# Down projection: the loads of the token tiles move from SP's queue to ScalarE's

## The chip, the cores and the metric

One Trainium2 chip; the kernel runs on 1 of its cores, and what counts is the device time of one launch in microseconds. TensorE multiplies, VectorE, ScalarE and GpSimd compute beside it, and SP (SyncE) issues DMAs. Each engine runs its own instruction list; semaphores order them. The time before is 1884.01 us, the median of 3 runs from 1882.34 to 1884.18.

## The reference, cut to what matters

The whole is one layer of a decoder for 1024 new tokens and 8 sampled ones, 1032 in all, in float32: a feed-forward half-step, a mixer (sliding-window attention beside HGRN2), and a second feed-forward half-step. The change touches the second product of both half-steps:

```
D_MODEL, D_FF = 1024, 2816

def half_step_ffn(x, g_pre, g_post, w_gu, w_down):
    h = rms_norm(x, g_pre)
    gate, up = jnp.split(h @ w_gu, 2, axis=-1)
    y = (jax.nn.silu(gate) * up) @ w_down
    return x + 0.5 * rms_norm(y, g_post)
```

`h @ w_down` is (1032 x 2816) times (2816 x 1024).

## The kernel before, in words

**Precision.** Every float32 factor is split in two parts of a shorter type: ScalarE copies the high part (`w_hi`, `x_hi`, also called `t_hi`), VectorE subtracts it from the original to get the low part (`w_lo`, `x_lo`). A product is three matmuls: high x high, high x low, low x high (L778 to L780).

**The down projection.** Tokens stand in three groups of 344. The product is computed with fewer multiplications in Strassen's manner: eleven streams, each a product of some combination of weight quarters with some combination of token quarters. Both kinds of combinations were formed in the gate and up stage and written to DRAM: token tiles to `spill_h`, weight sums to `spill_s`; some weights come directly from `w_down`. A stream has 11 blocks, so there are 121 blocks per half-step; a block is a weight tile of 128 x 512 (256 KB), a token tile of 128 x 344 (172 KB) and 12 matmuls. Two blocks make a pair: 61 pairs, numbered 0 to 60, the last with one block. There are two half-steps (`f` is 0 or 1), and so two such stages, from about 477 to 710 us and from about 1638 to 1870 us of the profiled execution.

**Buffers.** Raw weights of a pair go to `raw[p % 3]`, three slots; raw tokens to `t_raw`, eight tiles or four pairs deep. Their parts have as many slots. A pair's four transfers, two of weights and two of tokens, all count on one semaphore, `blocks_in[p % 4]`.

**The order of the work, written out by hand.** TensorE runs the blocks in order. In front of a pair it waits for `ab_low`, VectorE's count of finished pairs of low parts, and after each block it counts up `d_step`. ScalarE's loop (L1477) calls `high_parts(p)`: first the split of the tokens (L1417), then the split of the weights (L1406). Both wait in `landed(p)` until all four transfers of the pair are there; the weight split also waits on `d_step` until TensorE has finished pair p-3, whose slot it takes. Work of other kinds stands behind some pairs (`behind`, L1468 to L1476): copies of finished sums out of PSUM, squares and inverse roots for the norms, the input parts of the stage that follows. VectorE's loop does the low parts in the same manner (L2148, L2141).

**The loads.** All DMAs of this stage are issued by SP (L485 to L510). For each pair from 3 on, SP waits until the low parts of pair p-3 are done, so that the weight slot is free, issues the two weight loads (L461), waits until TensorE has finished pair p-4, whose token slot is taken, and issues the two token loads (L467). At a few pairs it also issues the last spills of the stage before (`last_out`), and from pair 12 to pair 27 six loads of the residual stream (L508); before pairs 4, 10, 11 and 20 it waits until those spills have been written that the coming tiles read (`t_out`, `odd_out`, `sums_out`). The tokens of pairs 1 to 3 are issued ahead of this loop (L484).

Of the kernel before, what the change touches and what calls it, by code (L numbers as in the profile page):

```python
# [21 lines left out]
KT = D_MODEL // P  # L22
# [13 lines left out]
FFN_STEPS = HT // 2  # L36
# [9 lines left out]
PAIR_STEPS = FFN_STEPS - 1  # L46
# [13 lines left out]
BLOCK_PAIRS = (BLOCKS + 1) // 2  # L60
LAST_PAIR = BLOCK_PAIRS - 1
COUNTED = BLOCKS - 1 + len((2, 3, 4, 5))
# [84 lines left out]
def tokens_of(k):  # L147

    s, i = divmod(k, FFN_STEPS)
    return (B11, T2, B21, T1, T3, B22, T4, E0, O0, E0, O0)[s], i  # L150


def slot_user(p):

    return p - 3


def pair_blocks(p):

    return range(2 * p, min(2 * p + 2, BLOCKS))  # L160
# [20 lines left out]
def build(nc, ins, outs):  # L181
    ctx = ExitStack()
    with ctx:
        sems = {}

        def sem(name):
            sems[name] = ctx.enter_context(nc.semaphore(name))
            return sems[name]
# [5 lines left out]
        def put(name, shape, dt, offset=None):  # L194
            size = (2 if dt == BF16 else 4) * int(np.prod(shape[1:]))
            if offset is None:
                offset = at[0]
                at[0] += (size + 31) // 32 * 32
            assert offset + size <= end, (name, offset + size - end)
            return nc.alloc_sbuf_tensor_at(name, shape, dt, offset=offset)  # L200
# [45 lines left out]
        t_raw = put("t_raw", [P, KT, GW], F32, x_at + 4 * NG * KT * GW)  # L246
# [86 lines left out]
        blocks_in = [sem(f"blocks_in{s}") for s in range(4)]  # L333
# [16 lines left out]
        S = sems  # L350
# [28 lines left out]
        def _(sp):  # L379
# [9 lines left out]
            def steps(n0, f, w_gu, w_down, x, first_load, late):  # L389

                done, hd, sums = FFN_STEPS * f, ins[f"spill_h{f}"], ins[f"spill_s{f}"]
# [62 lines left out]
                def weights_in(p):  # L454
                    for k in pair_blocks(p):
                        direct, summed_, i = weights_of(k)
                        src = w_down[direct[0]][:, direct[1]] if direct else sums[i][:, summed_]
                        if p == LAST_PAIR:
                            sp.dma_start(e_raw[:], src).then_inc(blocks_in[p % 4], 16)
                        else:  # L460
                            sp.dma_start(raw[p % 3][:, HALF * (k % 2):HALF * (k % 2 + 1)], src).then_inc(blocks_in[p % 4], 16)  # L461

                def tokens_in(p):
                    for k in pair_blocks(p):
                        op, i = tokens_of(k)
                        to, landed = (t_raw[:, k % KT], blocks_in[p % 4]) if p else (first_raw[:, k], S["first_in"])
                        sp.dma_start(to, hd[i][:, op]).then_inc(landed, 16)  # L467
# [17 lines left out]
                for p in range(3, BLOCK_PAIRS):  # L485
                    sp.wait_ge(S["ab_low"], BLOCK_PAIRS * f + slot_user(p) + 1)
                    if p == 4:
                        sp.wait_ge(S["t_out"], 16 * (done + PAIR_STEPS + f))
                        sp.wait_ge(S["sums_out"], 16 * (done + PAIR_STEPS + f) + 16)
                    if p == 10:  # L490
                        sp.wait_ge(S["t_out"], 16 * (done + FFN_STEPS + f))
                        sp.wait_ge(S["sums_out"], 16 * (done + FFN_STEPS + f) + 16)
                    if p == 11:
                        sp.wait_ge(S["odd_out"], 16 * (done + FFN_STEPS))
                    if p == 20:
                        sp.wait_ge(S["t_out"], 16 * (done + FFN_STEPS + f + 1))
                        sp.wait_ge(S["sums_out"], 16 * (done + FFN_STEPS + f + 1) + 16)
                    weights_in(p)
                    if p > 3:
                        sp.wait_ge(S["d_step"], COUNTED * f + 2 * (p - 4) + 2)  # L500
                        tokens_in(p)
                    if p in last_out:
                        last_out[p]()
                    for g, at_ in ((2, 12), (1, 18), (0, 24)):
                        for a in range(2):
                            if p == at_ + 3 * a:
                                t = slice(KT // 2 * a, KT // 2 * (a + 1))
                                sp.dma_start(resid[:, g, t], x[g][:, t]).then_inc(resid_full[g], 16)  # L508
                    if p in late:
                        late[p]()  # L510
# [7 lines left out]
            sp.dma_start(ident[:], ins["ident"]).then_inc(S["consts_in"], 16)  # L518
            sp.dma_start(head_ones[:], ins["head_ones"]).then_inc(S["consts_in"], 16)
            steps(0, 0, ins["w_gu1"], ins["w_down1"], ins["x"], 2, {53: lambda: store(0, outs["x1"], 0, 2)})  # L520
            sp.wait_ge(S["ab_low"], 58)
            sp.dma_start(raw[0][:], ins["w_in"][0]).then_inc(raw_full[0], 16)
# [742 lines left out]
        def _(act):  # L1265
# [8 lines left out]
            def square(n, src):  # L1274
                prior = [m for m in norms[:norm_no[n]] if sq_no[m] == sq_no[n]]
                if prior:
                    act.wait_ge(S["ss_done"], norm_no[prior[-1]] + 1)
                nc.scalar.activation(sq_bufs[sq_no[n]][:], src, ACT.Square, scale=D_MODEL ** -0.5).then_inc(S["sq_done"], 1)
# [27 lines left out]
            def ffn(u0, f, slot_uses, b):  # L1306
# [89 lines left out]
                def weights_high(p):  # L1396

                    landed(p)
                    if p == LAST_PAIR:
                        nc.scalar.activation(e_hi[:], e_raw[:], ACT.Copy).then_inc(S["ab_high"], 1)  # L1400
                        return
                    if p < 3:
                        act.wait_ge(S["p_done"], PRODUCTS * (last_pair + p // 2) + P4)
                    else:
                        act.wait_ge(S["d_step"], COUNTED * f + 2 * slot_user(p) + 2)
                    nc.scalar.activation(w_hi[p % 3][:], raw[p % 3][:], ACT.Copy).then_inc(S["ab_high"], 1)  # L1406

                def tokens_high(p):

                    if p:  # L1410
                        landed(p)
                        src = t_raw[:, 2 * p % KT:2 * p % KT + len(pair_blocks(p))]
                    else:
                        act.wait_ge(S["first_in"], 32 * (f + 1))
                        act.wait_ge(S["p_done"], PRODUCTS * (last_pair + 1) + UP)
                        src = first_raw[:]
                    nc.scalar.activation(t_hi[:, 2 * p % KT:2 * p % KT + len(pair_blocks(p))], src, ACT.Copy).then_inc(S["ab_high"], 1)  # L1417

                def high_parts(p):

                    tokens_high(p)
                    weights_high(p)
# [19 lines left out]
                def x_hi_half(g, a):  # L1442
                    r = rank_of(g)
                    if a:
                        act.wait_ge(S["x_new"], NG * b + r + 1)
                    else:
                        act.wait_ge(S["x_half_new"], NG * f + r + 1)
                    if g == 0:
                        act.wait_ge(S["d_step"], COUNTED * (f + 1))
                    high(b, g, a)  # L1450
# [10 lines left out]
                def gained(a):  # L1461
                    if a == 0:
                        act.wait_ge(S["y2_sq"], SQUARED + 1)
                    for m in range(KT // 2 * a, KT // 2 * (a + 1)):
                        st = nc.scalar.activation(y[:, 0, m], y[:, 0, m], ACT.Copy, scale=GAIN_F[b][:, m:m + 1])
                    st.then_inc(S["y_gained"], 1)
# [4 lines left out]
                if b == 0:  # L1471
                    behind.update({46: lambda: x_hi_half(2, 0), 47: lambda: x_hi_half(2, 1), 50: lambda: square(("S", 1, 2), resid[:, 2]),
                                   53: lambda: x_hi_half(1, 0), 54: lambda: x_hi_half(1, 1), 58: lambda: inverse(("S", 1, 2)),
                                   56: lambda: square(("S", 1, 1), resid[:, 1]), 59: square_lead})
                else:
                    behind.update({55: square_lead, 57: lambda: gained(0)})  # L1476
                for p in range(1, BLOCK_PAIRS):  # L1477
                    high_parts(p)
                    if p == 4:
                        act.preload_act_table_set("natural_log_exp_and_others")  # L1480
                    if p in behind:
                        behind[p]()
# [339 lines left out]
            square_x(2)  # L1822
            inverse(("S", 2, 2))
            ffn(U_FFN2, 1, [30, 30, 19, 11], 2)


# [1012 lines left out]
```

## Time and profile before

| what | before |
|---|---|
| median of 3 runs | 1884.01 us |
| profiled execution, own time | 1883.94 us |
| its span in the trace | 1882.1 us |
| TensorE busy | 1865.9 us (99%) |
| VectorE busy | 1371.2 us (73%) |
| ScalarE busy | 802.3 us (43%) |
| GpSimd busy | 35.1 us (2%) |
| mean DMA rate over the span | 158 GB/s |

The times of the table are of one execution, taken by the hardware profiler. Busy time is the union of an engine's instructions; issuing a DMA and waiting on a semaphore do not count as busy. Matmuls are pipelined: each is shown with some 320 ns, while the next one starts some 157 ns after it. "Idle before" is the time for which an engine stood still just before an instruction, and the releaser is what ended it. The share of the DMA engines is a mean over 16 of them.

### The profile page before, as it was taken

What the parts mean: (1) busy time and instruction counts of PE and PEld (TensorE: products, weight loads), DVE (VectorE), ACT (ScalarE), POOL (GpSimd) and SP (SyncE); (2) the same over time, 40 slices, a digit from 0 to 9 for tenths busy, and PEclk for the clock granted to TensorE, in tenths of its full rate; (3) what the DMA queues carried; (4) which work ended last, traced back from release to release, by engine and by line L of the source; (5) the groups of instructions that cost most, each with busy time, mean ns of one, the idle gap of its engine ahead of it and who ended that gap; (6) DMA issues with size and microseconds to landing.
All of it is one profiled execution on the core that took longest, in us unless ns stands there. A gap on an engine that the chain in (4) does not pass through costs nothing.

```text
span 1882.1 us, 36299 instructions
## 1 busy us (share of the span) xinstructions
PE 1865.9 (99%) x14325; PEld 1825.5 (97%) x14325; DVE 1371.2 (73%) x2132; ACT 802.3 (43%) x1278; POOL 35.1 (2%) x27
## 2 busy tenths in 40 slices
PE   9999999999999999999999999999999999999997
PEld 8999999999999999999898899999999999999997
DVE  7876767766756885578888678986776667766784
ACT  6423232323545673146565646522232223354553
POOL 0000000000000000000101100000000000000000
PEclk9999999999999999999999999999999999999999
DMA  5253433344798783210110465243434433598775
GB/s 191 79 191 123 149 127 141 123 162 155 260 313 254 224 270 106 64 40 25 36 30 31 143 242 171 85 171 126 145 123 154 149 140 126 178 315 294 227 242 181
DMA packets 115883, 296.60 MB, mean 158 GB/s; under 512 B 13200, under 2 KB 44824, under 8 KB 111160
## 3 DMA queue, kind: packets, MB, share of 16 engines
q1 hardware_dynamic: 115624, 294.93, 46.1%
q8 instruction: 84, 1.38, 0.3%
q14 instruction: 31, 0.25, 0.0%
q10 hardware_dynamic: 144, 0.03, 0.0%
HBM read 221.25 MB, written 73.00 MB: 156 GB/s over the span
## 4 chain that ended last, share of the span: by engine, by line
PE 94%; DVE 3%; ACT 1%; issue 1%; DMA 0%; DVEq 0%; SPq 0%; ACTq 0%
PE PS L669 9%; PE PS L671 9%; PE PS L670 9%; PE PS L778 8%; PE PS L780 8%; PE PS L779 8%; PE PS L678 5%; PE PS L679 5%; PE PS L680 5%; PE PS L901 2%; PE PS L902 2%; PE PS L903 2%; PE PS L642 2%; PE PS L644 2%; PE PS L643 2%; PE PS L1092 2%
## 5 line engine op out<-in xcount | busy, mean ns | idle before, releaser
L778 PE MATMUL PS<-x_hi,w_hi 128*128 128x344 f32 x960 | 309.2, 322 | 0.0
L780 PE MATMUL PS<-x_hi,w_lo 128*128 128x344 f32 x960 | 306.9, 320 | 0.0
L779 PE MATMUL PS<-x_lo,w_hi 128*128 128x344 f32 x960 | 306.6, 319 | 0.0
L1309 ACT ACTIVATE silu_g<-silu_g 128x344 f32<-128x344 f32 x92 | 45.0, 491 | 443.8 <-DVE silu_g L2121 258.9
L678 PE MATMUL PS<-x_hi,w_hi 128*128 128x344 f32 x640 | 204.7, 320 | 0.0
L679 PE MATMUL PS<-x_lo,w_hi 128*128 128x344 f32 x640 | 204.3, 319 | 0.0
L680 PE MATMUL PS<-x_hi,w_lo 128*128 128x344 f32 x640 | 203.8, 318 | 0.0
L778 PEld LDWEIGHTS PS<-x_hi,w_hi 128*128 128x128 f32 x960 | 180.4, 188 | 0.9
L2148 DVE TENSOR_TENSOR x_lo<-t_raw,x_hi 128x688 fp32r<-128x688 f32 x120 | 104.1, 867 | 105.9 <-ACT x_hi L1417 105.3
L779 PEld LDWEIGHTS PS<-x_lo,w_hi 128*128 128x128 f32 x960 | 180.3, 188 | 0.8
L780 PEld LDWEIGHTS PS<-x_hi,w_lo 128*128 128x128 f32 x960 | 180.3, 188 | 0.0
L1417 ACT ACTIVATE x_hi<-t_raw 128x688 fp32r<-128x688 f32 x120 | 92.7, 773 | 185.9 <-DMA t_raw<-spill_h 185.0
L1991 DVE TENSOR_TENSOR s_lo<-s_raw,s_hi 128x512 fp32r<-128x512 f32 x160 | 106.8, 688 | 82.2 <-ACT s_hi L1335 82.2
L1335 ACT ACTIVATE s_hi<-s_raw 128x512 fp32r<-128x512 f32 x160 | 100.8, 630 | 152.9 <-DVE s_raw L2098 138.9
L2141 DVE TENSOR_TENSOR w_lo<-raw,w_hi 128x1024 fp32r<-128x1024 f32 x120 | 146.8, 1224 | 13.0 <-ACT w_hi L1406 8.0
L669 PE MATMUL PS<-x_hi,w_hi 128*128 128x344 f32 x480 | 153.6, 320 | 0.9 <-DVE h_even L2118 0.7
L670 PE MATMUL PS<-x_sum,s_hi 128*128 128x344 f32 x480 | 153.9, 321 | 0.0
L671 PE MATMUL PS<-x_sum,s_lo 128*128 128x344 f32 x480 | 153.8, 320 | 0.0
L669 PE MATMUL PS<-x_sum,s_hi 128*128 128x344 f32 x480 | 153.7, 320 | 0.0
L671 PE MATMUL PS<-x_hi,w_lo 128*128 128x344 f32 x480 | 153.2, 319 | 0.0
L670 PE MATMUL PS<-x_lo,w_hi 128*128 128x344 f32 x480 | 152.8, 318 | 0.0
L1842 DVE TENSOR_TENSOR w_lo<-raw,w_hi 128x1024 fp32r<-128x1024 f32 x111 | 135.3, 1219 | 11.3 <-ACT w_hi L1272 7.0
(309 smaller groups left out, 4439.4 us busy)
## 6 DMA issues: line engine op xcount, KB each, us to landing
raw<-in_w_gu SPq DMA_DIRECT2D x88, 512.0 KB, 4.3
t_raw<-spill_h SPq DMA_DIRECT2D x238, 172.0 KB, 2.9
raw<-in_w_down SPq DMA_DIRECT2D x152, 256.0 KB, 3.6
d_raw<-in_w_down SPq DMA_DIRECT2D x44, 512.0 KB, 6.1
raw<-spill_s SPq DMA_DIRECT2D x88, 256.0 KB, 4.4
spill_s<-d_sum SPq DMA_DIRECT2D x20, 1024.0 KB, 5.1
spill_h<-T SPq DMA_DIRECT2D x20, 688.0 KB, 3.1
spill_h<-h_odd SPq DMA_DIRECT2D x22, 516.0 KB, 2.7
```

Of the source, the lines that this page charges most:

```text
L669: nc.tensor.matmul(PS[:, bank, :GW], wh[:, c], vh[:, k], start=(start and k == 0), stop=False, skip_group_check=not start)
L670: nc.tensor.matmul(PS[:, bank, :GW], wh[:, c], vl[:, k], start=False, stop=False, skip_group_check=not start)
L671: mm = nc.tensor.matmul(PS[:, bank, :GW], wl[:, c], vh[:, k], start=False, stop=(k == KT // 2 - 1), skip_group_check=not start)
L678: nc.tensor.matmul(PS[:, 7, :GW], wh, vh, start=(k == 0), stop=False)
L679: nc.tensor.matmul(PS[:, 7, :GW], wh, vl, start=False, stop=False)
L680: mm = nc.tensor.matmul(PS[:, 7, :GW], wl, vh, start=False, stop=(k == KT - 1))
L778: nc.tensor.matmul(PS[:, bank, :GW], hi[:, c], vh, start=opens, stop=False, skip_group_check=again)
L779: nc.tensor.matmul(PS[:, bank, :GW], hi[:, c], vl, start=False, stop=False, skip_group_check=again)
L780: mm = nc.tensor.matmul(PS[:, bank, :GW], lo[:, c], vh, start=False, stop=closes, skip_group_check=again)
L1842: nc.vector.tensor_tensor(w_lo[s][:], raw[s][:], w_hi[s][:].bitcast(F32), ALU.subtract)\
L1991: nc.vector.tensor_tensor(s_lo[k][:], s_raw[k][:], s_hi[k][:].bitcast(F32), ALU.subtract).then_inc(S["s_low"], 1)
L2141: return nc.vector.tensor_tensor(to[:], src[:], hi[:].bitcast(F32), ALU.subtract)
```

## The change

SP no longer issues the token loads of pairs 4 to 60, and no longer waits for `t_out`, `odd_out` and `d_step` there. ScalarE issues them: in the loop of pair p, after `high_parts(p)` and ahead of what stands behind the pair, it waits on `d_step` until TensorE has finished pair p-3 (that is (p+1)-4) and issues the two token loads of pair p+1 in its own queue. The waits for the spills move with them; that for the first `t_out` stands at pair 5, the first that reads such a tile. The token loads of pairs 1 to 3, the weight loads and all other transfers stay with SP. The four transfers of a pair still count on the same semaphore, and no size of a transfer or a buffer is changed.

```
                 for p in range(3, BLOCK_PAIRS):
                     sp.wait_ge(S["ab_low"], BLOCK_PAIRS * f + slot_user(p) + 1)
                     if p == 4:
-                        sp.wait_ge(S["t_out"], 16 * (done + PAIR_STEPS + f))
                         sp.wait_ge(S["sums_out"], 16 * (done + PAIR_STEPS + f) + 16)
                     if p == 10:
-                        sp.wait_ge(S["t_out"], 16 * (done + FFN_STEPS + f))
                         sp.wait_ge(S["sums_out"], 16 * (done + FFN_STEPS + f) + 16)
-                    if p == 11:
-                        sp.wait_ge(S["odd_out"], 16 * (done + FFN_STEPS))
                     if p == 20:
-                        sp.wait_ge(S["t_out"], 16 * (done + FFN_STEPS + f + 1))
                         sp.wait_ge(S["sums_out"], 16 * (done + FFN_STEPS + f + 1) + 16)
                     weights_in(p)
-                    if p > 3:
-                        sp.wait_ge(S["d_step"], COUNTED * f + 2 * (p - 4) + 2)
-                        tokens_in(p)
...
+                hd = ins[f"spill_h{f}"]
+
+                def tokens_in(p):
+
+                    done = FFN_STEPS * f
+                    if p == 5:
+                        act.wait_ge(S["t_out"], 16 * (done + PAIR_STEPS + f))
+                    if p == 10:
+                        act.wait_ge(S["t_out"], 16 * (done + FFN_STEPS + f))
+                    if p == 11:
+                        act.wait_ge(S["odd_out"], 16 * (done + FFN_STEPS))
+                    if p == 20:
+                        act.wait_ge(S["t_out"], 16 * (done + FFN_STEPS + f + 1))
+                    act.wait_ge(S["d_step"], COUNTED * f + 2 * (p - 4) + 2)
+                    for k in pair_blocks(p):
+                        op, i = tokens_of(k)
+                        act.dma_start(t_raw[:, k % KT], hd[i][:, op]).then_inc(blocks_in[p % 4], 16)
+
                 for p in range(1, BLOCK_PAIRS):
                     high_parts(p)
+                    if 3 < p + 1 < BLOCK_PAIRS:
+                        tokens_in(p + 1)
                     if p == 4:
                         act.preload_act_table_set("natural_log_exp_and_others")
                     if p in behind:
```

## Rows read from the trace of the kernel before

**Rows 1.** Page, part 1: busy us (share of the span) and instructions.
```profile
PE 1865.9 (99%) x14325; PEld 1825.5 (97%) x14325; DVE 1371.2 (73%) x2132; ACT 802.3 (43%) x1278; POOL 35.1 (2%) x27
```

**Rows 2.** Windows: busy time of each engine, PEclk, DMA share, GB/s.
```profile
480.00:590.00 110.00, 110.00 (x700) 109.95 (x699) 71.24 (x74) 54.20 (x65) 0.00 (x0) 1.00 0.89 293
590.00:700.00 110.00, 110.00 (x694) 109.21 (x693) 94.25 (x111) 73.20 (x88) 0.00 (x0) 1.00 0.76 238
1640.00:1750.00 110.00, 110.00 (x700) 109.95 (x699) 71.62 (x75) 55.21 (x64) 0.00 (x0) 1.00 0.89 291
...
1750.00:1858.00 108.00, 108.00 (x683) 107.40 (x682) 80.41 (x87) 61.02 (x71) 0.00 (x0) 1.00 0.77 242
```

**Rows 3.** Page, part 5: ScalarE's split of tokens, busy and idle time before.
```profile
L1417 ACT ACTIVATE x_hi<-t_raw 128x688 fp32r<-128x688 f32 x120 | 92.7, 773 | 185.9 <-DMA t_raw<-spill_h 185.0
```

**Rows 4.** Timeline of SP, 564 to 580 us: start, us, issues.
```profile
564.10 0.81 SPq L467 DMA_DIRECT2D t_raw<-spill_h  x2
...
567.89 2.21 SPq L467 DMA_DIRECT2D t_raw<-spill_h  x2
570.14 0.43 SPq L508 DMA_DIRECT2D resid<-in_x  x1
...
571.67 0.82 SPq L467 DMA_DIRECT2D t_raw<-spill_h  x2
...
575.46 0.81 SPq L467 DMA_DIRECT2D t_raw<-spill_h  x2
...
579.27 1.01 SPq L467 DMA_DIRECT2D t_raw<-spill_h  x2
```

**Rows 5.** Timelines of ScalarE and (last row) VectorE, 567 to 583 us.
```profile
567.55 0.78 ACT L1417 ACTIVATE x_hi<-t_raw 128x688 fp32r<-128x688 f32 x1 [0.52 <-DMA t_raw<-spill_h]
...
572.06 0.78 ACT L1417 ACTIVATE x_hi<-t_raw 128x688 fp32r<-128x688 f32 x1 [2.79 <-DMA t_raw<-spill_h]
...
578.30 0.78 ACT L1417 ACTIVATE x_hi<-t_raw 128x688 fp32r<-128x688 f32 x1 [4.51 <-DMA t_raw<-spill_h]
578.98 1.04 ACT L1406 ACTIVATE w_hi<-raw 128x1024 fp32r<-128x1024 f32 x1
580.53 0.78 ACT L1417 ACTIVATE x_hi<-t_raw 128x688 fp32r<-128x688 f32 x1 [0.51 <-DMA t_raw<-spill_h]
...
582.85 0.78 ACT L1417 ACTIVATE x_hi<-t_raw 128x688 fp32r<-128x688 f32 x1 [0.59 <-DMA t_raw<-spill_h]
...
580.06 1.22 DVE L2141 TENSOR_TENSOR w_lo<-raw,w_hi 128x1024 fp32r<-128x1024 f32 x1
```

**Rows 6.** DMA issues, 480 to 590 us: count, KB each, us to landing.
```profile
raw<-spill_s SPq DMA_DIRECT2D x44, 256.0 KB, 4.4
t_raw<-spill_h SPq DMA_DIRECT2D x58, 172.0 KB, 3.7
resid<-in_x SPq DMA_DIRECT2D x6, 688.0 KB, 5.8
```

**Rows 7.** Timelines of SP and VectorE at the start of the stage.
```profile
484.73 0.80 SPq L467 DMA_DIRECT2D t_raw<-spill_h  x2
...
496.10 0.80 SPq L467 DMA_DIRECT2D t_raw<-spill_h  x2
...
491.88 1.23 DVE L2141 TENSOR_TENSOR w_lo<-raw,w_hi 128x1024 fp32r<-128x1024 f32 x1
```

**Rows 8.** The DMA issue of ScalarE: ns min/median/max, first and last start.
```profile
L1507 ACTq DMA_DIRECT2D vecs<-in_vecs x1: 387/387/387, 0.9 to 0.9; - x1
```

**Rows 9.** Timeline of ScalarE, 680 to 683 us; no idle time in brackets.
```profile
680.21 1.99 ACT L1303 ACTIVATE x_hi<-resid,vecs 128x344 fp32r<-128x344 f32 x4
682.10 0.76 ACT L1417 ACTIVATE x_hi<-t_raw 128x688 fp32r<-128x688 f32 x1
```

**Rows 10.** Landing of t_raw in 480:590, then 590:700, then 1640:1750.
```profile
DMA to landing us min/median/max: 2.4/3.7/6.2
...
DMA to landing us min/median/max: 2.2/2.5/6.4
...
DMA to landing us min/median/max: 2.3/3.4/6.4
```

## The prediction

> **What bounds the kernel now.** I read the page's busy table first: TensorE is busy for 99% of the span and ScalarE for 43% [rows 1]. Then I cut both down projections into a first and a second stretch: in each TensorE is busy for all of its 110 us at a granted clock of 1.00, which is the 2.4 GHz level, and the waits of TensorE list nothing there [rows 2]. So inside the stage that the change touches there is no microsecond to win; whatever the edit does can only be hidden or cost time. The same rows show where the next limit stands: the DMA engines are at 0.89 in the first stretch (293 GB/s) and at 0.76 in the second. The grouped list then shows that ScalarE's split of token tiles has 185.9 us of idle time ahead of it, 185.0 of them until tokens land [rows 3]. This is the load that moves.
>
> How tight it is, from the timelines. SP issues the tokens of one pair at 564.10, 567.89, 571.67, 575.46 and 579.27 us, every 3.79 us, which is TensorE's time for a pair, since that wait counts its steps [rows 4]. ScalarE splits those pairs at 567.55, 572.06, 578.30, 580.53 and 582.85 [rows 5], so from the first issue of a pair to its split took 3.45, 4.17, 6.63, 5.07 and 3.58 us, mean 4.58. The 6.63 lies behind a resid load of 688 KB [rows 4, 6]. Tokens are issued when TensorE starts on the pair three before, that is 3 x 3.79 = 11.37 us ahead of use. The pair split at 578.30 has its low part done at 580.06 + 1.22 = 581.28 [rows 5], and TensorE starts on it at 571.67 + 11.37 = 583.04: 1.8 us of room in the worst of these. From split to low part done is 2.98 us. At the start of the stage (issue 484.73, low part done 493.11, needed at 496.10) the room is 3.0 us [rows 7].
>
> **The change, part by part.**
>
> Removed from SP: two token issues and three kinds of waits per pair. SP is nobody's limit, and its loads of weights now go out when the low part of pair p-3 is done, without standing behind the wait for a TensorE step. They come earlier. Cost and gain nothing: the tokens, not the weights, are what ScalarE waits for [rows 3].
>
> Added to ScalarE: 2 issues for each of 57 pairs in each of 2 projections. The one issue that ScalarE makes before took 0.387 us [rows 8]; 2 x 0.39 = 0.78 us a pair, on an engine that splits for 0.78 + 1.04 us of every 3.79 and idles for most of the rest [rows 5]. Hidden by that idle time; without cover it would be 0.78 x 114 = 89 us of ScalarE, not of TensorE. The spill waits (t_out, odd_out) count transfers issued many pairs before: nothing. The wait for TensorE's step in front of tokens p+1 has the same threshold as that of the weight split of p, which has just passed: nothing. Queued behind the added waits are the copies, squares and inverses of the stage, and they come after the issue.
>
> Moved, and this decides: before, SP issues tokens p+1 when TensorE has finished a pair, whether or not tokens p have landed, so two or three loads are in flight. After, the issue of p+1 stands behind both splits of p, and both of these wait for the landing of p. So only one token load is ever in flight, and the stage gets a loop of its own: issue, land, hand over both splits, issue again. If the loop L is under 3.79 us TensorE still sets the pace; above it every pair takes L - 3.79 out of the room, and then out of TensorE.
>
> L is D, from the first issue to the split, plus the step from split to the next issue. Bounds of that step: near zero if ScalarE's queue runs on while its splits compute, and 0.68 + 1.04 = 1.72 us if the issue waits for the end of the weight split [rows 5]. Rows speak for the first: a split starts at 682.10 without any gap behind activations that began at 680.21, although its wait for landing and others stand between them, and in rows 5 the weight split starts 0.68 us after a token split that lasts 0.78; ScalarE's waits are passed ahead of the work [rows 9]. I take 0.2 us: 0.1 for the hand-over and the rest for issues of 0.39 in place of 0.33.
>
> The Trainium skill (Perfetto Trace Analysis, section "Per-engine timelines") says that an ACT instruction is pushed into a wait queue and that the sequencer is then free, while a hardware DMA is worked off on the sequencer itself. Nothing in the trace of before shows a DMA behind a running activation, so no run here shows it yet; by this rule the step is the small one, by its opposite the third rival holds.
>
> D has bounds too. Below: in the second stretch the median landing is 2.5 us; with 0.37 between the two issues D = 2.87, L = 3.07, and nothing is lost there: under 3.79 it even gives room back. Above: D = 4.58 as in the sample of the first stretch, whose median landing is 3.7 (3.4 in the second projection) [rows 10]. Between them it hangs on the queues. The excess of 4.58 - 2.87 = 1.71 us came in one queue, where tokens wait for all that was issued before them. In a queue of their own they share the engines instead. At 293 GB/s for a share of 0.89 the engines move 329 GB/s when full [rows 2]; the 344 KB of a pair take 1.07 us alone and up to twice that beside a busy SP queue. In the first stretch SP's queue has 512 KB of weights a pair and 6.4 MB of resid loads and spills [rows 6]. With the full overlap of 1.07 I take D = 2.87 + 1.1 = 3.97 and L = 4.17 for the first projection: 0.38 us a pair over the 27 pairs (4 to 30) of the first stretch is 10.3, less the 3.0 of room: 7.3 us of TensorE. For the second projection, with landings shorter by 0.3, L = 3.87 and 0.08 x 27 = 2.2 stays within the room. Sum: +7.3 us.
>
> The Trainium skill (DMA: Bandwidth & Descriptors, "Issuing engines are not separate DMA queues") speaks against the change: loads issued from several engines interleave on the same 16 engines, and a second issuer saves only issue time. By it there is no bandwidth to win; no row of before shows two busy queues at once.
>
> The profiled execution took 1883.94 us for a span of 1882.1, and the median of the runs is 1884.01, so a term of the trace goes onto the median as it is: 1884.0 + 7.3 = 1891.3, say 1891.5.
>
> **The rivals.**
>
> Hidden altogether, the not-slower side. It decides at L = 3.79 in the first stretch, with 3.0 us of room for the sum. If sharing costs the tokens 0.7 us, not 1.1, L = 3.77. A bulk transfer delayed two or three overlapping token loads before and delays only one after. For: the minima of landing are 2.2 to 2.4 us even there [rows 10]. Against: the share of 0.89. Time: 1884, within 2.
>
> Landings stay as they were. If a second queue does not shorten the tokens' wait at all, L = 4.58 + 0.2 = 4.78 in the first projection: 0.99 x 27 - 3.0 = 23.7 us; in the second 0.69 x 27 - 3.0 = 15.6. Together +39: 1923. For: the engines are nearly full whoever issues. Against: the slower loop itself would relieve them.
>
> The issue waits for the computing splits. Then L = D + 1.72: 5.69 in the first stretch and 4.59 in the second: 1.9 x 27 + 0.8 x 29 - 3.0 = 71.5 us per projection, 143 in both: 2027. For: the program order. Against: rows 5 and 9.
>
> Faster: only by a tail or a seam that shifts by chance, as TensorE has no idle time here. 1880 at best.
>
> **How the numbers follow.** A difference of 0.2%, 3.8 us, is about the least that can be told from no change. Chances: forecast (some microseconds of stall, in the first stretches alone) 0.45, its own range 1888 to 1906; hidden 0.33; landings as before 0.12; serial issue 0.07; faster 0.03. So faster 0.03, same 0.33, slower 0.64. The range reaches from the hidden case, 1882, to the case of long landings, 1926; the serial case and some of the rest stay outside.
>
> **What would show it.** Right: the tokens' issues on ScalarE's queue start 0.1 to 0.2 us after a token split starts, not 3.79 us apart by TensorE's steps; their pitch in the first stretch is around 4.1 us until TensorE waits for w_lo in single gaps of some tenths, all before the 31st pair; and in the second stretch the pitch falls back to 3.79 with no gap. D there is under 3.6. Wrong: an issue that starts only 1.7 us after the split (then the stall runs through the stage), a D in the first stretch under 3.6 (then nothing is lost), or waits of TensorE anywhere outside the two projections.

## The result, and the profile after

| | before | changed |
|---|---|---|
| median | 1884.08 us | 1956.09 us |
| runs | 4, 1882.34 to 1884.18 | 4, 1955.02 to 1957.65 |
| span of the profiled execution | 1882.1 us | 1955.9 us |

The ratio is 1.0387, 95% interval 1.0374 to 1.0399: slower by 72 us, where 7 were forecast and the range ended at 1926. The direction was right, the size was not.

The page of the changed kernel, busy line (part 1), the two queues that carry the loads (part 3: packets, MB, share of the engines) and two groups of part 5:

```profile
PE 1890.5 (97%) x14325; PEld 1836.2 (94%) x14325; DVE 1372.5 (70%) x2132; ACT 799.2 (41%) x1278; POOL 35.1 (2%) x27
...
q1 hardware_dynamic: 83080, 255.11, 38.1%
q10 hardware_dynamic: 32688, 39.85, 6.6%
...
L770 PE MATMUL PS<-x_hi,w_hi 128*128 128x344 f32 x960 | 319.3, 333 | 49.1 <-DVE w_lo L2153 39.4
...
L1409 ACT ACTIVATE x_hi<-t_raw 128x688 fp32r<-128x688 f32 x120 | 92.8, 773 | 275.6 <-DMA t_raw<-spill_h 274.4
```

The number of instructions is that of before [rows 1]. TensorE has 49.1 us of idle time in front of the first matmul of a pair, where it had none, and its busy time is 24.6 us longer; the sum is the 73.8 us of span. ScalarE's idle time in front of the token split grew from 185.9 [rows 3] to 275.6 us. VectorE and ScalarE do the same work as before.

The windows that answer to [rows 2] (columns: PE, PEld, DVE, ACT, POOL busy, PEclk, DMA share, GB/s), and the waits of TensorE (total, times, longest):

```profile
480.00:590.00 110.00, 98.26 (x588) 94.92 (x588) 57.43 (x60) 43.75 (x52) 0.00 (x0) 0.97 0.76 245
590.00:720.00 130.00, 120.15 (x726) 116.22 (x725) 94.89 (x108) 69.58 (x85) 0.00 (x0) 0.97 0.68 216
1640.00:1750.00 110.00, 102.20 (x630) 100.17 (x629) 64.06 (x82) 43.37 (x55) 0.00 (x0) 0.98 0.69 222
...
PE PS L770 <- DVE w_lo L2153: 39.4, 32, 3.0
PE PS L770 <- ACT root L1279: 9.0, 2, 4.9
```

In the first 110 us of the stage 588 matmuls start, not 700. The DMA engines are less busy than before, 0.76 for 0.89, so they are not at a limit over the stretch as a whole. Besides the waits for low parts there are two of 4 to 5 us for a root that ScalarE computes, of which the prediction said nothing.

The loop itself, on the timeline of ScalarE in the changed kernel (start, us, engine; ACTq is its queue):

```profile
567.49 0.78 ACT L1409 ACTIVATE x_hi<-t_raw 128x688 fp32r<-128x688 f32 x1 [1.30 <-DMA t_raw<-spill_h]
567.58 0.82 ACTq L1485 DMA_DIRECT2D t_raw<-spill_h  x2
568.17 1.04 ACT L1398 ACTIVATE w_hi<-raw 128x1024 fp32r<-128x1024 f32 x1
572.80 0.78 ACT L1409 ACTIVATE x_hi<-t_raw 128x688 fp32r<-128x688 f32 x1 [3.59 <-DMA t_raw<-spill_h]
572.89 0.82 ACTq L1485 DMA_DIRECT2D t_raw<-spill_h  x2
573.48 1.05 ACT L1398 ACTIVATE w_hi<-raw 128x1024 fp32r<-128x1024 f32 x1
577.90 0.78 ACT L1409 ACTIVATE x_hi<-t_raw 128x688 fp32r<-128x688 f32 x1 [3.38 <-DMA t_raw<-spill_h]
...
616.79 0.78 ACT L1409 ACTIVATE x_hi<-t_raw 128x688 fp32r<-128x688 f32 x1 [2.06 <-DMA t_raw<-spill_h]
...
620.88 0.78 ACT L1409 ACTIVATE x_hi<-t_raw 128x688 fp32r<-128x688 f32 x1 [2.35 <-DMA t_raw<-spill_h]
620.97 0.82 ACTq L1485 DMA_DIRECT2D t_raw<-spill_h  x2
...
624.62 0.78 ACT L1409 ACTIVATE x_hi<-t_raw 128x688 fp32r<-128x688 f32 x1 [2.01 <-DMA t_raw<-spill_h]
```

The issue starts 0.09 us after the token split starts (567.58 after 567.49), while that split still runs for 0.7 us and before the weight split starts. The next split follows when the load has landed: 5.31 and 5.10 us later in the first stretch, 4.09 and 3.74 in the second. The pitch is the mean distance of these starts from pair to pair. In the first projection it is 4.76 us for pairs 4 to 30 (480.07 to 608.66, 27 pairs), 4.03 for 31 to 37, 4.19 for 38 to 51 and 5.00 for 52 to 60; in the second it is 4.79, 3.94, 4.24 and 4.56. TensorE needs 3.79.

Where the time went, from the starts of TensorE's first matmul of a pair, against before, each counted from pair 0 (us, first / second projection): by pair 31 +21.9 / +23.4; by pair 38 +23.1 / +24.5; by pair 40 +29.6 / +32.1; by pair 51 +29.6 / +32.1, nothing more; by pair 60 +34.4 / +39.3. The two sum to 73.7, the whole difference of the spans.

### The profile page after: what moved, and what is told of

Its sections match the earlier page's. It is cut to its first block, busy times and chain, and to the rows that moved or that the text cites. A ratio compares the mean times of both kernels' runs of the same rounds, so it can differ in the third digit from the quotient of the medians.

```text
span 1955.9 us, 36305 instructions
## 1 busy us (share of the span) xinstructions
PE 1890.5 (97%) x14325; PEld 1836.2 (94%) x14325; DVE 1372.5 (70%) x2132; ACT 799.2 (41%) x1278; POOL 35.1 (2%) x27
## 4 chain that ended last, share of the span: by engine, by line
PE 74%; DMA 16%; DVE 4%; ACT 2%; ACTq 2%; issue 2%; DVEq 0%; SPq 0%
DMA t_raw<-spill_h 16%; PE PS L661 9%; PE PS L663 9%; PE PS L662 9%; PE PS L670 5%; PE PS L671 5%; PE PS L672 5%; PE PS L770 3%; PE PS L772 2%; PE PS L893 2%; PE PS L771 2%; PE PS L894 2%; PE PS L895 2%; ACTq L1485 2%; PE PS L636 2%; PE PS L634 2%
## 5 line engine op out<-in xcount | busy, mean ns | idle before, releaser
L770 PE MATMUL PS<-x_hi,w_hi 128*128 128x344 f32 x960 | 319.3, 333 | 49.1 <-DVE w_lo L2153 39.4
L770 PEld LDWEIGHTS PS<-x_hi,w_hi 128*128 128x128 f32 x960 | 184.4, 192 | 63.2 <-DVE w_lo L2153 52.1
L1409 ACT ACTIVATE x_hi<-t_raw 128x688 fp32r<-128x688 f32 x120 | 92.8, 773 | 275.6 <-DMA t_raw<-spill_h 274.4
L670 PE MATMUL PS<-x_hi,w_hi 128*128 128x344 f32 x640 | 204.5, 320 | 0.0
L771 PEld LDWEIGHTS PS<-x_lo,w_hi 128*128 128x128 f32 x960 | 184.5, 192 | 0.9 <-issue 0.2
L661 PE MATMUL PS<-x_hi,w_hi 128*128 128x344 f32 x480 | 153.4, 320 | 0.8 <-DVE h_even L2130 0.7
```

Source lines behind the costliest of these rows:

```text
L661: nc.tensor.matmul(PS[:, bank, :GW], wh[:, c], vh[:, k], start=(start and k == 0), stop=False, skip_group_check=not start)
L670: nc.tensor.matmul(PS[:, 7, :GW], wh, vh, start=(k == 0), stop=False)
L770: nc.tensor.matmul(PS[:, bank, :GW], hi[:, c], vh, start=opens, stop=False, skip_group_check=again)
L771: nc.tensor.matmul(PS[:, bank, :GW], hi[:, c], vl, start=False, stop=False, skip_group_check=again)
```

## The experiments

Three theories stood at the start. One-in-flight: the loads of a pair are tied to the landing of the pair before. Shared-engines: two busy queues slow every load. Issue-time: issuing on ScalarE costs ScalarE's time. The count "in flight" needs a word of care. In the kernel before, the tokens of pair p+1 went out before those of pair p had landed for 17 of the 19 pairs 12 to 30 of the first projection, but for only 3 of the 21 pairs 31 to 51 (13 and 1 in the second projection). What the change adds everywhere is the tie: the next issue can't come before this landing.

**The issue ahead of the splits** (`ahead_of_split`). Only the order in ScalarE's loop is turned:

```
                 for p in range(1, BLOCK_PAIRS):
-                    high_parts(p)
                     if 3 < p + 1 < BLOCK_PAIRS:
                         tokens_in(p + 1)
+                    high_parts(p)
```

> The changed kernel with one order turned round: in ScalarE's loop the token loads of pair p+1 are issued ahead of the two splits of pair p, no longer behind them. Queue, engine, sizes and waits stay. Theory one-in-flight (the loads of p+1 are tied to the landing of p, so the stage runs at the pace of issue, landing, hand-over): with this order the loads are tied to TensorE's steps again, two are in flight, TensorE's idle time in the stages goes to under 1 us, and the time is 1884 to 1888. Rival shared-engines (two busy queues slow every load, wherever the issue stands): landings stay at 4 us and more and a good part of the loss stays, 1920 or more. Rival issue-time (0.8 us of issuing per pair on ScalarE is what hurts): nothing changes, 1950 to 1956.

Measured 1885.85 us against 1883.01 on the same chip, ratio 1.0013 (1.0004 to 1.0023): 70 of the 72 us are gone with the queue, the engine and the sizes as in the changed kernel. Its first stretch, its waits of TensorE in the stage, and its loads between 600 and 700 us (KB each, median us to landing):

```profile
480.00:590.00 110.00, 110.00 (x700) 109.95 (x699) 68.28 (x72) 52.66 (x63) 0.00 (x0) 1.00 0.87 293
...
PE PS L770 <- ACT root L1279: 0.5, 2, 0.4
...
PE PS L770 <- DVE w_lo L2153: 0.4, 1, 0.4
...
raw<-in_w_down SPq DMA_DIRECT2D x46, 256.0 KB, 3.5
t_raw<-spill_h ACTq DMA_DIRECT2D x49, 172.0 KB, 3.3
```

TensorE is busy for all of the 110 us again, with the 700 matmuls of [rows 2]. So the tie is what costs, and issue-time falls: the 2 issues per pair are still there. But the landing is 3.3 us where it was 2.5 in the second stretch [rows 10]. The loads are slower here too, and hidden, as their issue doesn't wait for the landing before.

**One in flight on SP's queue** (`sp_one_in_flight`), in the kernel before:

```
                         sp.wait_ge(S["d_step"], COUNTED * f + 2 * (p - 4) + 2)
+                        sp.wait_ge(S["ab_high"], 2 * (BLOCK_PAIRS * f + p - 1) + 1)
                         tokens_in(p)
```

> The kernel before, all loads on SP's queue, with one wait added: SP issues the tokens of pair p only when ScalarE has done the high part of the tokens of pair p-1. Theory one-in-flight: the queue does not matter, the tie does; the loop is a load (3.6 us in the second stretches to 4.6 in the first, as in the kernel before) plus 0.78 us of split and some 0.1 of hand-over, 4.5 to 5.5 us a pair against 3.79: 30 to 70 us per projection, 1945 to 2020 in all. Rivals shared-engines and issue-time: no second queue and no issue on ScalarE, so 1884 to 1890.

Measured 1938.66 us, ratio 1.0297 (1.0280 to 1.0314): 56 us slower with nothing but a tie, in the old queue, and 6 us under the low end of what was expected. The timelines of ScalarE and SP in it, and its loads between 600 and 700 us:

```profile
627.50 0.78 ACT L1418 ACTIVATE x_hi<-t_raw 128x688 fp32r<-128x688 f32 x1 [2.81 <-DMA t_raw<-spill_h]
...
631.18 0.78 ACT L1418 ACTIVATE x_hi<-t_raw 128x688 fp32r<-128x688 f32 x1 [1.94 <-DMA t_raw<-spill_h]
...
628.36 0.80 SPq L467 DMA_DIRECT2D t_raw<-spill_h  x2
629.21 0.91 SPq L461 DMA_DIRECT2D raw<-in_w_down  x2
632.03 1.71 SPq L467 DMA_DIRECT2D t_raw<-spill_h  x2
...
t_raw<-spill_h SPq DMA_DIRECT2D x49, 172.0 KB, 2.5
```

From split to next issue it takes 0.86 us here (627.50 to 628.36), 0.77 more than in the changed kernel, as the wait is on the end of the split. Even so it is faster than the changed kernel by 17 us, because a load lands in 2.5 us here and not in 3.2. From first issue to split the mean over pairs 12 to 30 is 3.86 us here and 4.53 in the changed kernel; over pairs 31 to 37 it is 3.16 and 3.90. With the kernel before and the changed one, the two runs make a square: queue of SP or of ScalarE, tied to the landing or not. In both columns the loads of SP's queue land 0.7 to 0.8 us sooner, and the time shows it only where the tie is. The square doesn't say why they do: the move also changed when the weights go out.

**Thin weight loads from pair 31 on** (`thin_weights`), in the changed kernel:

```
-                            sp.dma_start(raw[p % 3][:, HALF * (k % 2):HALF * (k % 2 + 1)], src).then_inc(...)
+                            n = 16 if p > 30 else HALF
+                            sp.dma_start(raw[p % 3][:, HALF * (k % 2):HALF * (k % 2) + n], src[:, 0:n]).then_inc(...)
```

> The changed kernel in which the weight loads of pairs 31 to 60 bring only the first 16 of 512 columns of each tile (the rest of the slot keeps old data, so this part of the product is not the reference's). Token loads, splits, waits and matmuls are untouched. In the changed kernel a token load takes 3.2 us to land there against 2.4 to 2.5 when it stands in SP's queue behind the weights. Theory shared-engines (in a queue of its own a token load is served side by side with the weight loads in SP's queue and pays for it): landings fall to 2.2 to 2.5 us, the first issue to the split from 3.9 to 2.9 us, the loop to 3.0, under the 3.79 of TensorE, which catches up and waits nowhere in pairs 33 to 51: the 34 to 39 us of loss per projection shrink to 24 to 28, total 1932 to 1940. Rival (ScalarE's queue is slower by itself, as 0.37 to 0.46 between its issues against 0.33 to 0.43 hint): landings stay at 3.1 or more and the loop at 4.0.

Measured 1927.39 us, ratio 1.0233 (1.0204 to 1.0263, 2 runs, against 1883.72 us beside them). Its loads and windows, and below them the loads of the changed kernel in the same window:

```profile
t_raw<-spill_h ACTq DMA_DIRECT2D x53, 172.0 KB, 2.4
...
480.00:590.00 110.00, 96.90 (x580) 93.79 (x579) 57.53 (x60) 43.81 (x52) 0.00 (x0) 0.97 0.75 244
590.00:700.00 110.00, 107.33 (x673) 106.01 (x673) 85.24 (x96) 65.59 (x78) 0.00 (x0) 1.00 0.44 126
```

```profile
raw<-in_w_down SPq DMA_DIRECT2D x44, 256.0 KB, 2.9
t_raw<-spill_h ACTq DMA_DIRECT2D x48, 172.0 KB, 3.2
```

With next to no weights beside them the tokens land in 2.4 us, as fast as in SP's queue, though they stand in ScalarE's. So the 0.8 us come from sharing the engines with the weights, not from the queue. From pair 31 to 37 the pitch of the splits is 3.25 us (3.41 in the second projection), ScalarE gets ahead, and the waits for the root are gone: the later part of the stage loses nothing, and what stays is the loss of pairs 4 to 30, 22.3 and 22.8 us by pair 38. The result is 5 us under the low end of what was expected.

**When the weights go out.** The traces of these runs show most of what the square leaves open. In the kernel before, SP issues the next weights right behind a pair of tokens, so the tokens that follow go out 2.9 us later (first two lines). In the changed kernel SP is free of the token loads and issues weights as soon as a slot is free, which is 2.92 us after an issue of tokens; at a loop of 4.0 us the next tokens follow only 1.1 us later. Below are such a pair and one whose issue a stall of TensorE held back, both from the second projection of the changed kernel, with the landing of their tokens (KB each, us):

```profile
591.42 0.90 SPq L461 DMA_DIRECT2D raw<-in_w_down  x2
594.33 0.80 SPq L467 DMA_DIRECT2D t_raw<-spill_h  x2
...
1845.50 0.80 SPq L461 DMA_DIRECT2D raw<-in_w_down  x2
...
1846.19 0.82 ACTq L1485 DMA_DIRECT2D t_raw<-spill_h  x2
...
t_raw<-spill_h ACTq DMA_DIRECT2D x2, 172.0 KB, 3.4
...
1849.11 0.80 SPq L461 DMA_DIRECT2D raw<-in_w_down  x2
...
1852.30 0.82 ACTq L1485 DMA_DIRECT2D t_raw<-spill_h  x2
...
t_raw<-spill_h ACTq DMA_DIRECT2D x2, 172.0 KB, 2.4
```

| pairs 31 to 51 of both projections | last weights issued before the tokens by | landing, first / second tile, median |
|---|---|---|
| before, 39 of 42 pairs | 2.3 us or more | 2.45 / 2.70 us |
| changed, 32 of 42 | under 1.5 us | 3.00 / 3.47 us |
| changed, 6 of 42 | 1.5 to 2.3 us | 2.73 / 3.25 us |
| changed, 3 of 42 | 2.3 us or more | 2.32 / 2.43 us |

The one pair that is left had weights issued 0.08 us behind its tokens, and took 3.47 / 4.27 us. So at the same distance behind the weights a load in ScalarE's queue was no slower than one in SP's, by 3 pairs here and 3 more in `root_at_39` (2.37 / 2.45 us); what the move lost is the distance. SP's queue does differ for weights that go out behind the tokens. Before, they follow after 0.85 us and do little harm. In `ahead_of_split` they follow in the other queue within 0.5 us for 21 of the 42 pairs, at 3.15 / 3.95 us; and 7 pairs with weights 0.5 to 1.3 us behind them took 2.37 / 3.39. No run holds the distance of before in the changed kernel, so how much of the 72 us it would give back is open.

**The root a pair earlier** (`root_at_39`), in the changed kernel. TensorE waits at pair 38 for a root that stands behind the splits of pair 40 in ScalarE's loop:

```
-                          40: lambda: inverse(("F", b, 2)), 43: ...
+                          39: lambda: inverse(("F", b, 2)), 43: ...
```

> The changed kernel with the inverse root of the first token group taken from behind pair 40 to behind pair 39 in ScalarE's loop. In its trace TensorE waits 4.2 and 4.9 us at the first block of stream E0 (pair 38) for that root, since ScalarE's lead over TensorE has shrunk and the root stands behind the splits of pair 40. Theory seam (this wait is a cost of its own, beside the loop): the wait falls by a loop of some 4 us each time, and with it the low clock behind it: 8 to 12 us, 1944 to 1948. Rival (the seam only gives the loop time that it would lose anyway, as a wait lets the loads run ahead): less than 4 us, 1952 to 1956.

Measured 1953.94 us, ratio 1.0373 (1.0355 to 1.0390), 2.2 us under the changed kernel: the rival was right. The waits of TensorE in it:

```profile
PE PS L770 <- DVE w_lo L2153: 43.2, 31, 5.5
...
PE PS L770 <- ACT root L1279: 1.3, 1, 1.3
```

The wait for the root fell from 9.0 to 1.3 us and that for low parts rose from 39.4 to 43.2. A stop at one place lets the loads run ahead, and the pairs behind it run on that lead: in the changed kernel TensorE loses nothing from pair 40 to 51, though the pitch of the splits stays above its pace (4.19 and 4.24 us for pairs 38 to 51). With the root moved, TensorE loses 2.8 and 2.3 us from pair 38 to 51, where it lost 6.5 and 7.6; but then it loses 9.1 and 7.8 from pair 51 to 60, where it lost 4.8 and 7.2. So of the cost between pairs 38 and 40 a good part was saved at first, and more than half of that was given back at the end.

**The residual loads later** (`resid_later`), in the changed kernel:

```
-                    for g, at_ in ((2, 12), (1, 18), (0, 24)):
+                    for g, at_ in ((2, 31), (1, 37), (0, 43)):
```

> The changed kernel with the six loads of the residual stream (688 KB each) at pairs 31 to 46 instead of 12 to 27. Theory (bulk transfers in SP's queue share the engines with the one token load and stretch the loop in the first stretch: 4.6 us a pair there, 4.0 without them): from pair 12 to 27 the loop falls from 4.6 to 4.0 or 4.1 us, and the same bulk makes pairs 31 to 46 longer, where the loop was 4.0, so the loss moves more than it shrinks: total within 8 us of 1956. Rival (the first stretch is slow because its weights come from the spilled sums, not for the bulk): the loop from 12 to 27 stays at 4.6, and 31 to 46 get longer too: 1965 or more.

Measured 1957.23 us, ratio 1.0391 (1.0374 to 1.0409), as slow as the changed kernel, within the 8 us expected. The pitch of pairs 12 to 30 fell from 4.63 to 4.41 us in the first projection and from 4.81 to 4.33 in the second, and that of pairs 31 to 37 rose from 4.03 to 4.84 and from 3.94 to 4.89. So bulk in SP's queue does stretch the loop, and moving it moves the loss. But the pitch of pairs 12 to 27 came to 4.30 and 4.23 us, not to the 4.0 or 4.1 expected. In pairs 12 to 30 the bulk explains 0.2 to 0.5 us of a pair, and some 0.4 stay over the 4.0 of pairs 31 to 37.

**All weights from `w_down`** (`direct_weights`), in the run before this one:

```
-                        src = w_down[direct[0]][:, direct[1]] if direct else sums[i][:, summed_]
+                        src = w_down[direct[0]][:, direct[1]] if direct else w_down[2 * i][:, 0:HALF]
```

> The run with the residual loads at pairs 31 to 46, and now every weight tile of the down projection is loaded from w_down, also where the product wants a sum of quarters from the spilled ones (so the product is not the reference's; sizes, counts and issues are the same). Left in pairs 12 to 30 of that run was a pitch of 4.4 us against 4.0 in the pairs 31 to 37 of the changed kernel. Theory (tiles of the spilled sums load more slowly or hold the engines longer): the pitch of 17 to 30 falls to 4.0 to 4.1. Rival (the rest comes from the spills that are still being written and from chance): it stays at 4.3 to 4.4.

Measured 1953.98 us, ratio 1.0374 (1.0344 to 1.0405, 2 runs). The pitch of pairs 17 to 30 is 4.00 us in the first projection, where it was 4.38, and 4.30 in the second, where it was 4.35. One projection speaks for the theory and the other against it, in one profile. Inconclusive: what holds the last 0.4 us of the pitch there is open.

## Why the prediction was wrong

**What held.** The bound was read rightly: inside the stage there was nothing to win. The mechanism was the forecast one: no issue before the landing of the pair before, a loop of issue, landing and hand-over, and a loss of pitch minus 3.79 for each pair, less the room at the start. With the measured pitch the sum of the prediction comes out: (4.76 - 3.79) x 27 - 3.0 = 23.2 us against 21.9 by pair 31 in the first projection, and (4.79 - 3.79) x 27 - 3.0 = 24.0 against 23.4 in the second. The spill waits and the issues on ScalarE cost nothing, as forecast; `ahead_of_split` has both.

**The step that failed** is the term D, from the first issue to the split. It said 3.97 us for the first stretch of the first projection, 3.67 for that of the second (L = 3.87, lost within the room), and 2.87 for the second stretch. The measured means are 4.85 (pairs 4 to 11) and 4.53 (12 to 30) in the first projection, 4.61 and 4.71 in the second, and 3.90 and 3.81 for pairs 31 to 37. So the second projection, which had 0 in the sum, lost as much as the first, and the second stretches, which were to give room back, gave none.

The reason stands in the sentence that the weights of SP "come earlier. Cost and gain nothing". Before, tokens went out 2.9 us behind the last weights, which land 3.5 us from their issue, so that they were nearly through; in the changed kernel they go out some 1.1 us behind them and share the engines with them, and the landings of the second stretch are longer by 0.7 us, 3.2 against 2.5. Thin weights take this away, and so does chance distance in the changed kernel itself. The 2.87 of the quiet stretch held for tokens 2.9 us behind the weights, and was carried over to a program in which nothing keeps that distance. In the first stretch full overlap was counted as 1.07 us on top of the least, with no term for a bulk transfer, behind which D reaches 6.96 us (pair 20, issued 0.6 us behind 688 KB).

A smaller error: "two or three loads are in flight" holds for the first stretch before, but hardly for the second, where D was 3.27 us (pairs 31 to 37). By this sum the tied loop, 3.27 + 0.09, would have stayed under 3.79 with the landings of before; there it is the longer landing that turned the tie into a loss.

The rule of the Trainium skill on the same point (DMA: Bandwidth & Descriptors, "Issuing engines are not separate DMA queues": the DMAs interleave on the same 16 engines) agrees with the trace, and it bears on more than was taken from it. It was read as "no bandwidth to win", but a load that interleaves with others also lands later: 3.2 us with full weights beside it, 2.4 with thin ones.

**What follows from D.** With D = 3.90 the loop of the second stretch is over 3.79 us, not under it. So it gives no room back, the lead of ScalarE over TensorE stays near nothing, and everything that relied on this lead shows: the root at pair 38, and the stores of 1376 KB near the end, behind which a load takes over 8 us (+4.8 and +7.2 us from pair 51 to 60). The forecast had the loss end at pair 30, which is where `thin_weights` has it end.

**The hand-over** of 0.2 us was of the right kind, and is 0.09 us. The trace agrees with the rule of the Trainium skill that was weighed there (Perfetto Trace Analysis, "Per-engine timelines"): ScalarE's DMA goes out while the split still computes (567.58 after 567.49). The serial rival, 1.72 us and 2027, is refuted by the same rows.

**The rivals.** "Hidden altogether" failed, at 3.79, for the same D. "Landings as they were", 1923, named a pitch of 4.78 for the first stretch of the first projection, close to 4.76, and 4.48 for that of the second, where it is 4.79. That it came near is luck: it took the landings of before, where two pairs were often in flight, and the changed kernel has one pair close behind weights. It had no loss in the second stretch and was wrong there.

**The clock.** I had no term for it. The windows of the changed kernel show it (column PEclk):

```profile
540.00:544.00 4.00, 4.00 (x18) 4.00 (x18) 1.24 (x2) 0.28 (x2) 0.00 (x0) 0.60 0.92 256
566.00:570.00 4.00, 2.50 (x9) 2.50 (x10) 3.01 (x4) 1.91 (x3) 0.00 (x0) 0.63 0.53 136
648.00:656.00 8.00, 4.81 (x17) 4.84 (x18) 4.45 (x5) 4.37 (x6) 0.00 (x0) 0.57 0.58 182
...
1734.00:1738.00 4.00, 4.00 (x17) 4.00 (x16) 2.10 (x2) 1.16 (x2) 0.00 (x0) 0.57 0.79 244
1761.00:1765.00 4.00, 3.05 (x11) 3.05 (x12) 3.00 (x3) 1.72 (x2) 0.00 (x0) 0.59 0.50 152
1847.00:1854.00 7.00, 5.60 (x20) 5.63 (x21) 5.07 (x6) 3.58 (x5) 0.00 (x0) 0.51 0.65 212
```

At or behind some stalls (1.9, 3.0 and 4.2 us long in the first projection) TensorE stood at the 1.2 GHz level, where it never did in this stage before [rows 2]. In the first three windows that is 3.2, 3.0 and 6.9 us, in the last three 3.4, 3.3 and 6.9; at half the rate it costs at most half of these 26.7 us, 13.4 of the 24.6 us of longer busy time. About 5 us more are no work at all: in front of a stall the last matmul is shown for 0.32 us, and the next could have started after 0.16, some 30 times. What the low level cost in time was not separated by a run, as part of it would have been waiting for loads anyway; but between pairs 38 and 40 half of the 6.9 us and the wait of 4.2 for the root give 7.6, near the +6.5 of that place.

## What to carry to other kernels

Before a load is moved into another engine's program, ask what its issue stood behind there and what it will stand behind here: an issue behind the consumer of the load before can't come before that load has landed, and then the landing time, which was hidden, is part of the pace. Turning two lines round, so that the issue comes ahead of the consumer, gave back 70 of 72 us. And look at the loads that stay behind: with the urgent ones gone from their program, they go out at other times, and may come to lie just in front of the urgent ones.

## What the runs showed of the hardware that was not expected

The landing of a load hangs on how long before it another was issued, more than on the queue: 172 KB land in 2.5 us when 512 KB of weights went out 2.9 us earlier, in 3.2 when they went out about 1 us earlier, and in 2.4 when they are thin. A stop of TensorE is partly given back: a wait of 4 to 5 us for a root bought the pairs from 40 to 51 at full pace, and its removal saved 2.2 us in all.
